# A decay matrix of the Mamba-2 scan from one product with a strict triangle and one exponential; the first tile without a zero state

## What is computed

```python
adt = (dt * a).reshape(b, nc, Q, G, R)
acum = jnp.cumsum(adt, axis=2).transpose(0, 1, 3, 4, 2)
cb = jnp.einsum('bclgn,bcsgn->bcgls', cc, bc)
# seg_decay: exp(acum[l] - acum[s]) where s <= l, else 0
lmat = seg_decay(acum)
y_diag = jnp.einsum('bcgls,bcgrls,bcsgrp->bclgrp', cb, lmat, xd)
...
h0 = jnp.zeros((b, G, R, P, N), jnp.float32)
# state before chunk c: h = h * exp(acum[-1]) + states[c]
y_off = jnp.einsum('bclgn,bcgrpn,bcgrl->bclgrp', cc, prev, jnp.exp(acum))
```

## Time and profile before

| what | value |
|---|---|
| median of 3 runs | 3841.83 us (3838.88 to 3861.46) |
| the profiled execution | 3885.88 us |
| its span, first to last instruction | 3884.1 us |
| busy: PE, DVE, ACT, POOL | 3107.9, 2827.4, 1032.1, 2189.7 us |
| busy share: PE, DVE, ACT, POOL | 80%, 73%, 27%, 56% |
| mean granted TensorE clock | 0.904 of full speed |
| moved by DMA | 1394.61 MB, mean 359 GB/s |

### The profile page before, as it was taken

How to read it: one execution, slowest core, us unless ns; L and a number is a source line. 1 busy time by engine, 2 the same in 40 slices (tenths; PEclk the granted TensorE clock), 3 DMA queues, 4 the chain that set the end, 5 groups by cost and what they waited for, 6 DMA issues and landing times.

```text
span 3884.1 us, 41019 instructions
## 1 busy us (share of the span) xinstructions
PE 3107.9 (80%) x13528; PEld 2275.1 (59%) x13528; DVE 2827.4 (73%) x5879; ACT 1032.1 (27%) x2585; POOL 2189.7 (56%) x1839
## 2 busy tenths in 40 slices
PE   8984888888899878998987878888887865565655
PEld 8874876677777537786764547767764522121221
DVE  3338856988866887787777778768776876667666
ACT  5512532243412214443212114333311110011101
POOL 0005534665554776676556787557656777455553
PEclk9997989998899999999999999989998997777787
DMA  6568999999898999999899999989999999999997
GB/s 238 195 249 337 403 382 368 385 364 340 334 340 328 360 343 369 381 395 376 337 409 367 362 351 402 356 340 375 348 381 384 322 349 356 421 421 421 421 421 327
DMA packets 316546, 1394.61 MB, mean 359 GB/s; under 512 B 35376, under 2 KB 40880, under 8 KB 251824
## 3 DMA queue, kind: packets, MB, share of 16 engines
q0 software_dynamic: 262656, 1073.86, 71.7%
q1 hardware_dynamic: 52384, 313.42, 20.6%
q10 hardware_dynamic: 1296, 4.72, 0.3%
HBM read 1387.66 MB, written 4.19 MB: 358 GB/s over the span
## 4 chain that ended last, share of the span: by engine, by line
PE 36%; DMA 16%; POOL 11%; issue 8%; DVE 6%; ACT 2%; DVEq 1%; another core or an unknown queue 1%; ACTq 0%; POOLq 0%
PE main L555 15%; POOL rowbuf L515 10%; PE vbank L641 5%; DMA rowbuf<-euv,idx 4%; DMA rowbuf<-ev,idx 4%; PE main L563 3%; DMA ring<-euv,idx 3%; PE turn L626 3%; DVE acc L1550 2%; PE main L764 2%; PE main L749 2%; DVE rowbuf L1524 2%; DMA xT<-euv,idx 2%; DMA merged<-euv,idx 2%; DMA late<-euv,idx 1%
## 5 line engine op out<-in xcount | busy, mean ns | idle before, releaser
L515 POOL DMA_INDIRECT rowbuf<-eu,idx x800 | 995.7, 1245 | 912.8 <-DVE hdot L1524 430.6
L1524 DVE CUSTOM_DVE_ANT_0 rowbuf<-rowbuf,hb 128x1024 f32<-128x1024 f32 x884 | 1078.6, 1223 | 216.0 <-DMA rowbuf<-eu,idx 110.9
L515 POOL DMA_INDIRECT rowbuf<-ev,idx x800 | 907.7, 1135 | 462.4 <-issue 220.0
L641 PE MATMUL vbank<-rowbuf,vdiag 128*128 128x512 f32 x1436 | 755.5, 663 | 259.6 <-DMA rowbuf<-ev,idx 185.6
L555 PE MATMUL main<-xT,ring 128*128 128x256 f32 (+1 forms) x4480 | 824.4, 343 | 84.7 <-ACT mm L998 39.9
L555 PEld LDWEIGHTS main<-xT,ring 128*128 128x128 f32 x4480 | 726.7, 194 | 177.0 <-issue 107.2
L1550 DVE SCALAR_TENSOR_TENSOR acc<-rowbuf,hact,acc 128x1024 f32<-128x1024 f32 x525 | 675.5, 1287 | 84.3 <-DMA rowbuf<-ev,idx 65.8
L641 PEld LDWEIGHTS vbank<-rowbuf,vdiag 128*128 128x128 f32 x1436 | 281.7, 210 | 663.6 <-issue 512.4
L954 ACT ACTIVATE vdiag<-ident,hact 128x128 f32<-128x128 f32 x441 | 163.4, 396 | 566.6 <-DVE hact L1533 346.3
L749 PE MATMUL main<-late,ring 128*128 128x256 f32 (+1 forms) x1280 | 240.3, 352 | 36.6 <-issue 27.8
L749 PEld LDWEIGHTS main<-late,ring 128*128 128x128 f32 x1280 | 214.4, 202 | 61.8 <-issue 31.4
(11 more groups left out here) (223 smaller groups left out, 3576.7 us busy)
## 6 DMA issues: line engine op xcount, KB each, us to landing
ring<-wblocks SPq DMA_DIRECT2D x280, 1024.0 KB
rowbuf<-eu,idx POOLq DMA_INDIRECT x800
rowbuf<-ev,idx POOLq DMA_INDIRECT x800
pw<-poolw SPq DMA_DIRECT2D x20, 256.0 KB
h_out<-acc ACTq DMA_DIRECT2D x8, 512.0 KB
xT<-xt SPq DMA_DIRECT2D x3, 1024.0 KB
zy<-x SPq DMA_DIRECT2D x3, 1024.0 KB
craw_ln<-ln1g SPq DMA_DIRECT2D x5, 512.0 KB
```

The costliest lines, as they stand in the source:

```text
L515: pool.indirect_dma_start(rows[r], None, (eu, ev)[table], bass.IndirectOffsetOnAxis(ap=idx[c % 2][:, u, k:k + 1], axis=0)).then_inc(row_re ...
L641: last = pe.matmul(vbank[half][:, :], vdiag[:, n % DIAGS, :], r[:, half * 512:(half + 1) * 512], start=first, stop=False, skip_group_check ...
L1524: last = dve.tensor_tensor_reduce(r, r, hb[c % 2][:, t, :], 1.0, 0.0, ALU.mult, ALU.add, hdot[:, g % 2, k:k + 1])
```

## The change

The exponent of a decay is now made as a sum over the tokens between s and l: `upper` scaled a head by `adt` (four ScalarE copies with a scale into `lexp`, `log_steps`) is multiplied by TensorE with the strict triangle `below`, in one fp32 product of 512 columns, and one exponential of 512 columns without a bias, from PSUM into the same `lexp` buffer, replaces the four. The exponents above the diagonal come out as 0 and not as a large negative number, so the mask goes onto the scores: VectorE reads them from PSUM and multiplies them with `upper` into `cbs`, in place of ScalarE's copy. The copies to `adtc` and the bf16 constants go. `scan_scores` now waits for ScalarE (`steps_made`), and the copies wait for VectorE's `gates_read` and for the `lexp` buffer (`m_done`). In the first tile (the first eight steps) the carried state is zero: TensorE leaves out C times the state, and VectorE gates the output straight from PSUM and copies the new state.

```diff
--- before.py
+++ after.py
-        mask = sb("mask", [P, P])
-        ident_short, mask_short = sb("ident_short", [P, P], BF16), sb("mask_short", [P, P], BF16)
-        mask4 = mask_short[:, :].unsqueeze(1).to_broadcast([P, HG, P])
+        below = sb("below", [P, P])
...
-        adtc = sb("adtc", [P, NT, 2 * HG])
...
-        adtc_ready = sem("adtc_ready")
+        gates_read, steps_made = sem("gates_read"), sem("steps_made")
...
-            pool.affine_select(out=mask[:, :], in_=mask[:, :], compare_op=ALU.is_ge, fill=NEG, base=0,
-                               pattern=[[1, P]], channel_multiplier=-1).then_inc(const_made, 1)
+            pool.affine_select(out=below[:, :], in_=below[:, :], compare_op=ALU.is_gt, fill=0.0, base=0,
+                               pattern=[[-1, P]], channel_multiplier=1).then_inc(const_made, 1)
...
@@ -583,15 +580,10 @@
 
             def scan_scores(c, j, s):
 
-                t, gg = s // 2, s % 2
                 lbank = bank(c, j * MA, DECAYS[s])
-                pe.matmul(lbank[:, :], ident_short[:, :], mask4, start=True, stop=False,
-                          skip_group_check=True)
-                for h in range(HG):
-                    last = pe.matmul(lbank[:, h * P:(h + 1) * P],
-                                     adtc[:, t, gg * HG + h:gg * HG + h + 1].to_broadcast([P, P]), upper[:, :],
-                                     start=False, stop=(h == HG - 1), skip_group_check=True)
-                last.then_inc(l_ready, 1)
+                pe.wait_ge(steps_made, scans(c, j, s) + 1)
+                pe.matmul(lbank[:, :], below[:, :], lexp[:, s % 2, :, :].rearrange("p h l -> p (h l)"),
+                          start=True, stop=True).then_inc(l_ready, 1)
...
-                pe.matmul(ybank[:, GW:2 * GW], CT[:, gg, t * P:(t + 1) * P],
-                          state[:, ds(j * 2 * GW + gg * GW, GW)], start=True, stop=False, skip_group_check=True)
+                begun = n >= 2 * AJ
+                if begun:
+                    pe.matmul(ybank[:, GW:2 * GW], CT[:, gg, t * P:(t + 1) * P],
+                              state[:, ds(j * 2 * GW + gg * GW, GW)], start=True, stop=False, skip_group_check=True)
                 for ct in range(2):
                     pe.matmul(ybank[:, ct * P:(ct + 1) * P], xs[:, 2 * gg + ct, t * P:(t + 1) * P],
-                              ddiag[:, 2 * gg + ct, :], start=False, stop=False, skip_group_check=True)
+                              ddiag[:, 2 * gg + ct, :], start=not begun and ct == 0, stop=False, skip_group_check=True)
...
-                pe.wait_ge(adtc_ready, c * AJ + j + 1)
-                unturned(pe, c, j * TA + 8)
                 scan_scores(c, j, 0)
                 for s in range(2 * nt):
                     if s < 2 * nt - 1:
...
                 until(o(20))
-                for t in range(nt):
-                    act.copy(cbs[:, 2 * t:2 * t + 2, :],
-                             turned(c, j * TA, 8 + t)[:, 0:2 * P].rearrange("p (g l) -> p g l", g=2)).then_inc(turn_free, 1)
+
+            def log_steps(c, j, s):
+                n = scans(c, j, s)
+                act.wait_ge(gates_read, c * AJ + j + 1)
+                act.wait_ge(m_done, n + 1)
+                t, gg = s // 2, s % 2
+                for h in range(HG):
+                    last = act.activation(lexp[:, s % 2, h, :], upper[:, :], ACT.Copy,
+                                          scale=adt[:, ds(t * HEADS + j * 2 * HG + gg * HG + h, 1)])
+                last.then_inc(steps_made, 1)
 
             def decays(c, j, s):
                 n = scans(c, j, s)
                 act.wait_ge(l_ready, n + 1)
-                act.wait_ge(m_done, n + 1)
-                t, gg = s // 2, s % 2
                 lbank = main[mains(c, j * MA + DECAYS[s]) % BANKS]
-                for h in range(HG):
-                    last = act.activation(lexp[:, s % 2, h, :], lbank[:, h * P:(h + 1) * P], ACT.Exp,
-                                          bias=nacum[:, ds(t * HEADS + j * 2 * HG + gg * HG + h, 1)])
-                last.then_inc(main_free, 1)
+                act.activation(lexp[:, s % 2, :, :].rearrange("p h l -> p (h l)"), lbank[:, :], ACT.Exp).then_inc(main_free, 1)
 
             def front_a3(c, j):
                 o = place(c, j * PA)
                 steps = 2 * CHUNK[c]
+                for s in range(2):
+                    log_steps(c, j, s)
                 for s in range(steps):
                     until(o((20, 21, 23, 26)[s]))
+                    if s >= 2:
+                        log_steps(c, j, s)
                     decays(c, j, s)
                     if s == 1:
                         silu_z(c, j, 1)
...
             def merge_pool(c, j):
                 unturned(dve, c, j * TA + 3)
                 tc = CHUNK[c] * P
-                dve.tensor_tensor(merged[:, ds(j * 2, 2), 0:tc], asb[:, :, 0:tc], gps[:, :, 0:tc], ALU.mult)
-
-                for t in range(CHUNK[c]):
-                    last = dve.tensor_copy(adtc[:, t, :], adt[:, ds(t * HEADS + j * 2 * HG, 2 * HG)])
-                last.then_inc(adtc_ready, 1)
+                dve.tensor_tensor(merged[:, ds(j * 2, 2), 0:tc], asb[:, :, 0:tc], gps[:, :, 0:tc], ALU.mult
+                                  ).then_inc(gates_read, 1)
                 yield
...
@@ -1332,7 +1327,19 @@
                 y3 = yt1[:, :].rearrange("p (h d) -> p h d", h=HG)
                 dve.drain()
                 st = state[:, ds(j * 2 * GW + gg * GW, GW)]
+                y = yg[:, t, gg * GW:(gg + 1) * GW]
+                z = zs[:, t, gg * GW:(gg + 1) * GW]
                 dve.wait_ge(y_ready, n + 1)
+                if n < 2 * AJ:
+                    if s == 1:
+                        emptied(dve, c, j * MA + 10)
+                    dve.tensor_tensor(y, ybank[:, 0:GW], z, ALU.mult).then_inc(gated, 1)
+                    dve.wait_ge(st_ready, n + 1)
+                    dve.tensor_copy(st, stbank[:, 0:GW]).then_inc(st_used, 1)
+                    dve.wait_ge(gated, n + 1)
+                    dve.sem_inc(y_free, 1)
+                    yield
+                    return
                 dve.tensor_tensor(y3, ybank[:, GW:2 * GW].rearrange("p (h d) -> p h d", h=HG),
                                   spread(heads(eacum, t, j, gg), HD), ALU.mult)
...
                 yield
                 dve.drain()
-                y = yg[:, t, gg * GW:(gg + 1) * GW]
                 if s == 1:
                     emptied(dve, c, j * MA + 10)
-                dve.tensor_tensor(y, yt1[:, :], zs[:, t, gg * GW:(gg + 1) * GW], ALU.mult).then_inc(gated, 1)
+                dve.tensor_tensor(y, yt1[:, :], z, ALU.mult).then_inc(gated, 1)
                 yield
...
             def scan(c, j):
                 unturned(dve, c, j * TA + 8)
+                for t in range(CHUNK[c]):
+                    dve.wait_ge(turn_ready, turns(c, j * TA + 8 + t) + 1 + TURNED)
+                    dve.tensor_tensor(cbs[:, 2 * t:2 * t + 2, :],
+                                      turn[turns(c, j * TA + 8 + t) % BANKS][:, 0:2 * P].rearrange("p (g l) -> p g l", g=2),
+                                      upper[:, :].unsqueeze(1).to_broadcast([P, 2, P]), ALU.mult).then_inc(turn_free, 1)
+                dve.drain()
                 yield from scan_pre(c, j, 0)
...
             dve.wait_ge(const_made, 11)
-            dve.tensor_copy(ident_short[:, :], ident[:, :])
-            dve.tensor_copy(mask_short[:, :], mask[:, :])
```

2 lines of the change are left out of this document (1 added, 1 removed).

## The result

The changed kernel takes 3912.22 us (median of 4 runs, 3899.75 to 3918.15) and the kernel before, on the same chip, 3847.84 (4 runs, 3838.88 to 3861.46): a ratio of 1.0151, 95% interval 1.0112 to 1.0190. (One of the six runs behind 1.0106 took 4335 us, at a granted clock of 0.716 instead of 0.91, and is left out of that ratio.) So the kernel is slower by 1.0 to 1.5%; the three intervals overlap. The forecast had the direction right, and with 19.5 us a half to a third of the size. 3912 lies outside the range of 3830 to 3892; with the 39 to 40 us of the two later measurements it would have been 3887 to 3889, inside.

A forecast was written before the change was run, and what follows sets the result against it. Scans were taken as bounded by a TensorE-ScalarE-VectorE chain, with no engine full. Terms -1 + 1.5 + 6.4 + 2.4 + 7.2 + 3 = 19.5 us, added to the median of 3841.83, gave 3861 us; range 3830 to 3892.

The forecast's parts named there:

- TensorE's relief: Score products: 15 us less TensorE work, counted as nothing in the sum; as a rival on the path, 3827 us, chance 0.10.
- Step 0 in superchunk 0: First tile's scans: eight scaled copies before the table load make the first step 1.1 us later each round.
- Step 0 in the scan of superchunk 3: Copies, table load and exponential make VectorE's first product 0.8 us later; eight such rounds in superchunks 3 and 4, 6.4 us.
- Step 2 there: Copies behind the activation of z make the exponential 0.7 us later; 11 rounds by 0.65, 7.2 us.
- The last round there: End of superchunk 0: gated output about 1.5 us sooner, with two VectorE operations instead of five; first tile together -1 us.
- Step 0 in the later rounds: Superchunks 2 to 4: eight waiting rounds lose 0.8 us each, 6.4 us; four others pay 0.6 for masked scores, 2.4 us.
- What stands behind the new wait: Row sums and outputs queued behind TensorE's wait at step 2: 0.5 to 1 us more in five rounds, 3 us together.
- the clock and the ring: Scans: TensorE's wait lowers its clock and row buffers run short, 40 us more, 3900 us; chance 0.14.
- The first, that transfers swallow the loss: Projections behind each scan: DMA is the true limit, so later scans lose nothing; 3837 to 3848 us, chance 0.22.
- The third: Scans: TensorE's new wait for ScalarE lowers its clock, 2 us a round, plus the ring's 2 us; 3900 us, chance 0.14.
- the chain: Scans: the dependency from TensorE's scores over ScalarE and VectorE back to TensorE's outputs, 8 to 35 us slower, chance 0.54.
- my own point: Wait behind the z block: the clock falls once it reaches some 3 us, which it does in superchunk 4.

The follow-up runs named there:

- the two later measurements: The changed kernel, unaltered, measured again against the kernel before on a second and third chip: ratios 1.0106 and 1.0102.
- the kernel that relieves clock and gathers: The changed kernel with TensorE's row sums moved ahead of the product of step 2: 3825.17 us, ratio 1.0080.
- the one that relieves the clock alone: The changed kernel with two or three useless TensorE products ahead of the wait of step 2: 3826.7 us, ratio 1.0081.
- the own buffer: The changed kernel with the scaled copies in a separate buffer, all made ahead: 3818.83 us, 0.9974; again on the third chip 3793.94 us, 0.9995.

## Why the prediction was wrong in size

**What held.** The product holds TensorE for 0.85 us at full clock (2650.16 to 2651.01; I took 0.86), and the 15 us of TensorE's relief worth nothing. Step 0 in superchunk 0 was to be late by 1.1 us: VectorE's product comes 4.3 us behind the end of the copy of B (43.20 to 47.49), before 3.2 (44.0 to 47.24), thus 1.1. Step 0 in the scan of superchunk 3: from the start of the copies to the product 4.37 us, before 3.40, thus 1.0 where I had 0.8. Step 2 there: 0.62 where I had 0.7. The outputs of step 1: 1.45 later, where the two terms gave 1.2 to 1.7. ScalarE's 33 us, TensorE's idle of 2 to 4 us at step 2 (1.94 and 3.76): as said. The three gaps of superchunk 0 grow by 3.1 us, 1.0 a round. The last round there didn't gain its 1 us. One sign of being wrong was that VectorE's waits for outputs fall. In the line for `yt` they do, 31.2 to 20.5, but only because the first tile's waits moved to another line; together they rose to 40.8.

**Step 0 in the later rounds** was too cheap. I had VectorE either wait for ScalarE or pay the masked scores, 0.8 or 0.6 us a round, for the three gaps of superchunk 2 some 2 us. They grow by 4.3, 4.2 and 3.7 us in three executions, by 1.9 with the masked scores alone, and not at all with the copies ahead (177.8 and 177.7 against 178.5). By that a round pays about 1.3 us and the copies count there too. In superchunks 3 and 4 the profile before is too disturbed for a comparison.

**The step that failed** is "What stands behind the new wait", with the step 2 before it. The two stood with 3 + 7.2 us in my sum; the clock and the ring were left out of it, for a rival of 0.14 and for the range. Of the sum's terms the scans hold just these two, and they are longer by 19.8, 14.9 and 20.5 us in three executions of the changed kernel, about twice the 10.2. Taking the copies of step 2 out gives back 22 to 24 us by the controls, and a us of later copies costs 1.6 (0.8 to 2.2), where I had one for one.

What the runs show in place of the 3 us is this. TensorE's product or the row sums behind its wait run below full clock in six, five and seven of the eight rounds of superchunks 3 and 4 (three executions; before, in none). Keeping TensorE busy in the wait gives back 7 to 10 us. The ring of 12 buffers doesn't cover 2 to 4 us, as I had it: GpSimd's longest idle times about step 2 go from 26.1 us to between 53 and 57 in eight rounds. That this costs time of its own isn't shown, since the kernel that relieves clock and gathers is no faster than the one that relieves the clock alone. The parts overlap, so they aren't a sum that closes. What a scan loses is not won back behind it: with the copies made twice the scans grew by 21.5 us, and the projections between them didn't shrink.

The measured 3912 us has 64 us of loss. What is shown here bears on the 38 to 40 us of the two later measurements; the 24 to 26 beyond them stay open.

**The rivals.** The first, that transfers swallow the loss, is out: the time rose in all three measurements. The second, TensorE's relief, is out, or worth under 0.2%, by the own buffer on the third chip (0.9995 [0.9981, 1.0008]), where the relief is there and no new wait is. The third named what happened, in kind and in place, but its size and its condition don't hold. It had 40 us on top of the chain, 24 for the clock and 16 for the ring, 3900 us in all; the clock measured 7 to 10, the ring nothing apart from it, and the whole excess is 38 to 40 on two chips. That 3900 is the forecast nearest to the measured 3912 is in good part luck. Nor is some 3 us of wait the point from which it acts: in the changed kernel's profile rounds with 2.23 us have it and others don't. The clock should have stood in the sum for the rounds of superchunk 4, where my own point was passed by the earlier trace rows. Its chance of 0.14 was too low for a mechanism that came true in part.

**What I hadn't seen.** I priced step 0 in superchunk 0 as late, rightly, but not what it is worth early. With nothing beside it, each round there pays ScalarE's whole order. VectorE's eight products of this superchunk, first to last, are 122.0 us apart before (47.2 to 169.2), 122.6 after and 115.5 with the copies ahead:

```profile
L1319 DVE TENSOR_TENSOR mm<-lexp,cdiag x8: 683/689/693, 47.5 to 170.1; 128x512 f32<-128x512 f32 x8
```

```profile
L1322 DVE TENSOR_TENSOR mm<-lexp,cdiag x8: 684/690/694, 46.2 to 161.7; 128x512 f32<-128x512 f32 x8
```

The first layer norm starts at 247.9 us before and at 236.6 and 235.3 with all copies ahead. So the idea of the change has 11 to 12 us to give up to there once its copies are early. Part of it needs no new exponent at all: the kernel before, with only the scores moved to VectorE, starts that norm at 245.2.

**Open.** Why the first measurement showed 1.0151 for the kernel that has 1.0106 and 1.0102 later. The intervals overlap, and both profiles of that pair have slow projections that the later ones don't have (505.2 and 494.1 us against 444.4 and 446.3), so the swings of that pair are large and not the change's; what sets them isn't shown. Open too is why the own buffer is only level with the kernel before although it wins those 11 to 12 us: what it gives back in the later superchunks is smaller than the swings between two executions, and wasn't tried.

## What to carry to other kernels

When an edit makes one in-order engine wait for another, list everything queued behind the waiting instruction and follow each item to who frees buffers by it: here a wait of 2 to 4 us for four small copies held row sums and gathers and lowered TensorE's clock, and a us of it cost 1.6. Here the next stage, with TensorE and DMA at full, won nothing back of what the scan ahead lost, so put such costs into the sum and not into the range. When a measured sum agrees with the forecast, check that both hold the same terms. And before giving up a rewrite that costs, move its preparatory work to where its engine idles: the same arithmetic was 1% slower with its copies late and level with the kernel before with all of them early.
